# Hybrid MoE step on one core: the samples' rows held as 128 partitions by 256, and half a weight row taken out of the ring

## The chip, the cores and the metric

The kernel runs on one core of one Trainium2 chip. The metric is the device time of one execution in microseconds (us), and lower is better. The kernel before took 1020.41 us, the median of three runs (1020.08 to 1020.62).

## The reference, cut to what matters

There are 288 token rows of 1024 columns: 256 of one prompt and 32 of samples (8 sequences of 4). A mixing layer makes `x`. The expert layer then dominates, with 32 experts whose two weight matrices are 8 MB and 4 MB of float32 each, about 400 MB in all:

```python
logits = xt.astype(jnp.float32) @ router_w.astype(jnp.float32) + router_b.astype(jnp.float32)
vals, idx = lax.top_k(logits, TOP_K)
...
for e in range(N_EXPERTS):
    gu = xt @ w1[e] + b1[e]
    gate = jnp.minimum(gu[:, :D_FF], SWIGLU_LIMIT)
    lin = jnp.clip(gu[:, D_FF:], -SWIGLU_LIMIT, SWIGLU_LIMIT)
    glu = gate * jax.nn.sigmoid(SWIGLU_ALPHA * gate)
    out = (glu * (lin + 1.0)) @ w2[e] + b2[e]
    acc = acc + combine[:, e:e + 1] * out
...
y_prompt = rmsnorm(hp, final_norm_g)
y_sample = rmsnorm(hs, final_norm_g)
```

`rmsnorm(x, g)` is `x * rsqrt(mean(x * x) + eps) * g`, over the 1024 columns of a row.

## The kernel before

Five programs run side by side, one for each engine's queue, and meet at semaphores. SyncE (SP) issues nearly all loads, TensorE (PE) multiplies, ScalarE (ACT) and VectorE (DVE) work on PSUM, GpSimd (POOL) helps at the front and raises the mean square to the power -1/2.

**Front.** The mixing layer ends in `x1_t`, the rows transposed. PE adds up router logits and row sums of squares in four column groups of 32 PSUM partitions (`route`, `add_square`), ACT copies them (`logit_parts`), PE turns the rows back to natural layout (`turn_x1(n, t)`, n the half of the columns, t the tile of rows: 0 and 1 are the prompt, 2 is the 32 samples). The routing chain goes from the logits over DVE, POOL and DVE to `mask`, to the ranks on PE, and to `place_first` on DVE, with which `gather_first` picks rows. Ahead of the ranks PE runs five small matmuls of `keep_awake`. ACT copies the left halves of the turned tiles to `x_acc` (`copy_half`) and makes normed rows (`norm_left`), DVE copies the right halves. `x_acc` is the accumulator of the output: tiles 0 and 1 fill 128 partitions by 1024, tile 2 fills 32 partitions by 1024.

**Pairs.** Experts go in 16 pairs. A w1 block of 512 rows of one expert is a unit of 4 MB: partition p holds its rows 4p to 4p+3, 8 KB each. Four units of 4 MB form `ring`; SP waits on `used` (PE has finished a unit), then loads the next into the freed slot. Within the first pair (`direct`) and the second, PE reports rows and half units (`row_used`, `half_used`), and `load_second` refills in halves. Apart from the ring, rows 0 and 1 of a unit of pair 14 lie in `held` and rows 0 and 1 of one of pair 13 in `late`, both loaded at the front; the ring load of that unit then begins at row 2 (`kept=True`). The front's own ring loads are `load_step(i, a)`: unit i, half a. The last of them, `load_step(3, 1)`, waits until all six `turn_x1` have been done.

A period works on one pair: `first_product` (pairs of 64-column groups in float32), `turn_back` (the places, for the way back), `gather` for the next pair, `second_product` of the pair before. The results of the pair before go back to their rows in six `spread_tile`s: j = 3c + t for half c of the columns and tile t, each two matmuls (`y_high`, `y_low`) of 512 columns into PSUM bank 6 or 7, which DVE adds to `x_acc` (`add_spread`).

**End.** The last units come in halves and column parts (`load_w2_rows`, `load_w2_columns`), then `gain_final` (512 KB, a broadcast of the norm's gain). `finish` on PE seeds PSUM with the four prompt tiles of `x_acc`, runs the last products and returns tiles in `LAST_ORDER` = (0, 1, 2, 5, 3, 4), each in its own bank. ACT squares each tile as it arrives and adds up the row sums; DVE adds the two sample tiles first and multiplies two prompt tiles by the gain (L1791); DVE (L1860) and POOL (L1917) make `rms`; ACT (L1454) and DVE (L1867) scale; six stores go out, the samples' last (L659).

## Time and profile before

| what | value |
|---|---|
| median of three runs | 1020.41 us |
| profiled execution, its own time | 1020.11 us |
| its span, first to last instruction | 1018.4 us |
| granted TensorE clock, mean | 0.985 of full speed |
| PE busy | 952.3 us (94%) |
| DVE, ACT, POOL busy | 311.5, 168.2, 73.5 us |
| read from HBM | 418.62 MB, 413 GB/s over the span |

The profiled execution lies 1.7 us outside its span and 0.30 us below the median. Busy time says how long an engine had work in flight, not whether it set the pace: that is read from what ended its idle time.

### The profile page before, as it was taken

How to read it: one execution, taken by the hardware profiler on the slowest of the kernel's cores; microseconds unless marked ns; L12 is line 12 of the kernel's file. 1: busy time of each engine (PE TensorE's matmuls, PEld its weight loads, DVE VectorE, ACT ScalarE, POOL GpSimd, SP SyncE). 2: the span in 40 equal slices, each digit the busy share in tenths (PEclk: the TensorE clock that was granted, in tenths of full speed). 3: DMA queues.
4: the chain of work that ended last, by engine and by line, in shares of the span. 5: the costliest groups of instructions: out<-in, count | busy, mean ns of one | idle time of the engine just before them, and what ended most of it. 6: DMA issues, size and time to landing. Idle time of an engine off the chain costs nothing.

```text
span 1018.4 us, 12465 instructions
## 1 busy us (share of the span) xinstructions
PE 952.3 (94%) x5216; PEld 428.6 (42%) x5216; DVE 311.5 (31%) x536; ACT 168.2 (17%) x354; POOL 73.5 (7%) x63
## 2 busy tenths in 40 slices
PE   8999999999988998989899898989899899999996
PEld 7999444343333433333243333324243334343332
DVE  5898622131303132231312222121313213131212
ACT  5355612101010101010020101002010101010012
POOL 5985000000000000000000000000000000000000
PEclk9999999999999999999999999999999999999998
DMA  9979999999999999999999999999999999999995
GB/s 322 322 297 411 358 421 437 432 422 435 422 436 425 434 430 430 432 425 437 427 436 431 430 431 424 434 427 435 426 435 432 422 436 423 437 423 433 420 422 202
DMA packets 31189, 420.47 MB, mean 413 GB/s; under 512 B 4219, under 2 KB 4763, under 8 KB 12454
## 3 DMA queue, kind: packets, MB, share of 16 engines
q1 hardware_dynamic: 30651, 418.70, 97.5%
q10 hardware_dynamic: 498, 1.24, 0.3%
q8 instruction: 26, 0.43, 0.2%
q14 instruction: 14, 0.11, 0.0%
HBM read 418.62 MB, written 1.49 MB: 413 GB/s over the span
## 4 chain that ended last, share of the span: by engine, by line
DMA 51%; PE 47%; issue 1%; SPq 0%; DVE 0%; POOL 0%; ACTq 0%; POOLq 0%; ACT 0%; DVEq 0%
DMA ring<-in_exp_w 50%; PE psum L953 22%; PE psum L971 8%; PE psum L760 2%; PE psum L761 2%; PE psum L762 2%; PE psum L1023 1%; PE psum L988 1%; PE psum L859 1%; PE psum L1024 1%; PE psum L794 1%; PE psum L793 1%; PE psum L792 1%; PE psum L842 1%; DMA rows_all<-in_x_sample 1%; PE psum L1006 1%
## 5 line engine op out<-in xcount | busy, mean ns | idle before, releaser
L953 PE MATMUL psum<-ring,rows_all 128*64 128x512 f32 x2016 | 461.6, 607 | 39.8 <-DMA ring<-in_exp_w 39.4
L953 PEld LDWEIGHTS psum<-ring,rows_all 128*64 128x64 f32 x2016 | 139.2, 139 | 316.8 <-issue 259.3
L971 PE MATMUL psum<-ring,rows_all 128*64 128x512 f32 x896 | 199.7, 599 | 13.3 <-DMA ring<-in_exp_w 13.3
L971 PEld LDWEIGHTS psum<-ring,rows_all 128*64 128x64 f32 x896 | 67.8, 138 | 136.4 <-issue 136.1
L1366 ACT ACTIVATE rows_all<-rows_all 128x512 f32<-128x512 f32 x32 | 20.1, 630 | 527.6 <-DVE rows_all L1723 527.6
L1711 DVE TENSOR_TENSOR rows_all<-rows_all,psum 128x512 f32<-128x512 f32 (+1 forms) x84 | 53.6, 678 | 172.2 <-PE psum L1024 172.2
L1740 DVE SCALAR_TENSOR_TENSOR y_low<-psum,gate_of,y_high 128x512 fp32r<-128x512 f32 x32 | 23.7, 751 | 245.8 <-ACT y_high L1374 245.6
L1723 DVE TENSOR_SCALAR rows_all<-psum 128x512 f32<-128x512 f32 x32 | 22.1, 692 | 193.4 <-PE psum L953 193.4
L1914 POOL TENSOR_TENSOR rows_all<-rows_all,held 32x512 f32<-32x512 f32 x1 | 1.3, 1272 | 909.1 <-DVE rows_all L1786 909.1
L1374 ACT ACTIVATE y_high<-psum,gate_of 128x512 fp32r<-128x512 f32 x32 | 22.0, 688 | 217.2 <-PE psum L971 191.0
L859 PEld LDWEIGHTS psum<-place,x_thirds 128*128 128x128 bf16 x744 | 46.6, 97 | 13.0 <-issue 13.0
L859 PE MATMUL psum<-place,x_thirds 128*128 128x128 bf16 x744 | 50.8, 219 | 0.0
L1297 ACT ACTIVATE rows_all<-psum,vecs 128x128 f32<-128x128 f32 x128 | 36.7, 368 | 19.0 <-PE psum L861 13.5
L762 PE MATMUL psum<-x_parts,w_low 128*128 128x288 f32 x128 | 37.7, 295 | 0.0
L1023 PE MATMUL psum<-y_high,back 128*128 128x512 f32 (+1 forms) x84 | 36.4, 433 | 0.0
L1730 DVE SCALAR_TENSOR_TENSOR rows_all<-psum,rows_all 128x512 f32<-128x512 f32 x32 | 33.8, 1056 | 1.1
L1024 PE MATMUL psum<-y_low,back 128*128 128x512 f32 (+1 forms) x84 | 33.1, 394 | 0.0
L1023 PEld LDWEIGHTS psum<-y_high,back 128*128 128x128 f32 (+1 forms) x84 | 13.5, 160 | 37.0 <-issue 34.1
L1902 POOL TENSOR_TENSOR w_low<-ring,w_high 128x512 fp32r<-128x512 f32 x19 | 27.5, 1467 | 13.1 <-ACT w_high L1218 13.1
L861 PE MATMUL psum<-place,samples_thirds 96*128 96x128 bf16 x124 | 27.4, 221 | 0.0
L762 PEld LDWEIGHTS psum<-x_parts,w_low 128*128 128x128 f32 x128 | 24.0, 188 | 0.0
L760 PE MATMUL psum<-x_parts,w_high 128*128 128x288 f32 x80 | 24.0, 300 | 0.0
(263 smaller groups left out, 761.9 us busy)
## 6 DMA issues: line engine op xcount, KB each, us to landing
ring<-in_exp_w SPq DMA_DIRECT2D x53, 4096.0 KB, 30.3
ring<-in_exp_w SPq DMA_DIRECT2D x75, 2048.0 KB, 25.5
ring<-in_exp_w SPq DMA_DIRECT2D x16, 1024.0 KB, 25.5
ring<-in_w_in SPq DMA_DIRECT2D x3, 2048.0 KB, 19.9
ring<-in_w_out SPq DMA_DIRECT2D x1, 4096.0 KB, 12.8
held<-in_exp_w SPq DMA_DIRECT2D x1, 2048.0 KB, 11.8
rows_all<-in_exp_w SPq DMA_DIRECT2D x1, 2048.0 KB, 14.5
ring<-in_exp_w SPq DMA_DIRECT2D x4, 512.0 KB, 21.8
```

Source lines behind the costliest of these rows:

```text
L760: mm(out, w_h, x_h, start=(k == 0), stop=False, skip_group_check=True)
L762: last = mm(out, w_l, x_h, start=False, stop=(k == KD - 1), skip_group_check=True)
L859: mm(out, x_thirds[:, t, part, own], place[:, t], start=(k + t + part == 0), stop=False, skip_group_check=True)
L861: return mm(out, samples_thirds[0:3 * NS, own], place[0:3 * NS, 2], start=False, stop=True, skip_group_check=True)
L953: last = mm(psum[c * SLOTS:(c + 1) * SLOTS, bank, :], gathered_t[:, 4 * kk + j, e, :], weights[:, j, (2 * g + c) * BANK:(2 * g + c + 1) * ...
L971: last = mm(psum[e * SLOTS:(e + 1) * SLOTS, 4 + c, :], h_t[:, 4 * i + j, e, :], ring_w2[:, slot, e, j, c * BANK:(c + 1) * BANK], start=Fal ...
L1023: mm(psum[0:rows[t], 6 + j % 2, :], z, y_high[:, c, :], start=True, stop=False)
L1024: mm(psum[0:rows[t], 6 + j % 2, :], z, y_low[:, c, :], start=False, stop=True).then_inc(spread, 1)
L1297: return A(gathered_t[:, k], src.rearrange("p (e n) -> p e n", e=2), ACT.Copy, scale=vecs[:, G_OWN + k:G_OWN + k + 1])
L1711: V.tensor_tensor(x_acc[0:rows[t], t, c * BANK:(c + 1) * BANK], x_acc[0:rows[t], t, c * BANK:(c + 1) * BANK], psum[0:rows[t], 6 + j % 2, : ...
L1730: V.scalar_tensor_tensor(out=gate_act[:, e, :].rearrange("p (j q) -> p q j", j=4), in0=psum[:, 2 + e, :].rearrange("p (q j) -> p q j", j=4 ...
L1902: G.tensor_tensor(w_low[:, c // KD, c % KD, :], w_in_sb[:, c // KD, c % KD, :], high_buffer(c).bitcast(F32), ALU.subtract).then_inc(w_low_ ...
```

## The change

The samples' 32 rows by 1024 columns are held as 128 partitions by 256: partition 32q + r has columns 256q to 256q+255 of row r (`samples_acc`, in the place of the router weights, `router_g`, once these are used up). PE's four column groups of 32 write them: `return_rows` makes them one tile of a period in place of two, in eight float32 matmuls of 256 columns (four groups, for `y_high` and for `y_low`), so that a period has `SPREADS` = 5 tiles in place of 6. At the front eight more float32 matmuls by the identity put the samples in that form (bank 2), between `turn_x1(0, 1)` and `turn_x1(0, 2)`, and ACT copies them (`copy_groups`) in place of `copy_half(2)`; `x1_turned` counts one more, and DVE copies two right halves in place of three.

The row of 4 KB per partition that `x_acc` gives up becomes `late_half`: half of row 2 of the unit of pair 13 whose rows 0 and 1 are in `late`. It is loaded (512 KB) at the front, behind `logit_parts_ready` and ahead of `load_step(3, 1)`. The ring load of that unit shrinks from 2 MB to 1.5 MB (`load_behind_half`).

At the end the samples' sum of squares is spread over four partitions for each row; one small PE step with `pick_table` adds the four and gives the sum to all four (`samples_meaned`, bank 5). The samples' gain needs its own layout, so four more loads of 32 KB (`gain_samples`) follow `gain_final`; DVE waits for all five before its first use of a gain. POOL no longer multiplies samples by the gain, ACT scales two tiles in place of three, DVE scales the samples first, and their store goes out first.

```diff
         x_norm = rows_all[:, 0:2]
-        x_acc = rows_all[:, 3:6]
+        x_acc = rows_all[:, 3:5]
+        late_half = rows_all[:, 5]
...
+        samples_acc = flat_router[:, 0:QUARTER]
...
+        gain_samples = held[:, 0, D:D + QUARTER]
...
-        LAST_BANKS = (2, 3, 4, 6, 7, 5)
-        LAST_SEEDS = (0, 1, 3, 4)
-        LAST_ORDER = (0, 1, 2, 5, 3, 4)
-        FINAL_DVE = (3, 4, 5)
-        FINAL_ACT = (0, 1, 2)
-        GAINED_DVE = (0, 1)
+        TILES = ((0, 0), (0, 1), (1, 0), (1, 1))
+        SAMPLES = len(TILES)
+        SPREADS = SAMPLES + 1
+        LAST_BANKS = (2, 3, 6, 7, 4)
+        MEAN_BANK = 5
+        LAST_SEEDS = (0, 1, 2, 3)
+        LAST_ORDER = (0, 1, SAMPLES, 2, 3)
+        FINAL_DVE = (2, 3)
+        FINAL_ACT = (0, 1)
...
+            def load_late_half():
+
+                rows = exp_w1[0][PAIRS * 2 - 6, 0:4 * P, :]
+                nc.sync.dma_start(late_half, rows.rearrange("(p j) n -> p j n", j=4)[:, 2, 0:D]).then_inc(late_half_landed, 16)
+
+            def load_behind_half(pair, slot):
+
+                rows = exp_w1[0][bass.ds(pair * 2, 1), 0:4 * P, :]
+                nc.sync.dma_start(ring_flat[:, slot, 5 * D:8 * D],
+                                  rows.rearrange("e (p j) n -> p (e j n)", j=4)[:, 5 * D:8 * D]).then_inc(landed[slot], 16)
...
             load_step(2, 0)
-            sp.wait_ge(x1_turned, 2 * NTILE)
+            sp.wait_ge(logit_parts_ready, 1)
+            load_late_half()
+            sp.wait_ge(x1_turned, 2 * NTILE + 1)
             load_step(3, 1)
...
             nc.sync.dma_start(gain_final, final_norm_g[None, :].to_broadcast([P, D])).then_inc(g_final_landed, 16)
+            for q in range(4):
+                nc.sync.dma_start(gain_samples[q * NS:(q + 1) * NS],
+                                  final_norm_g[None, q * QUARTER:(q + 1) * QUARTER].to_broadcast([NS, QUARTER])
+                                  ).then_inc(g_final_landed, 16)
...
             turn_x1(0, 1)
+            for k in range(2):
+                for q in range(4):
+                    last = mm(psum[q * NS:(q + 1) * NS, GROUPS_BANK, k * P:(k + 1) * P], x1_t[:, 2 * q + k, NP:T],
+                              ident[:], start=True, stop=True, skip_group_check=True)
+            last.then_inc(x1_turned, 1)
             turn_x1(0, 2)
             for t in REST_ORDER:
                 turn_x1(1, t)
-            keep_awake(5, ident[:], bank=7)
+            pe.wait_ge(x_half_copied, 1)
+            keep_awake(5, ident[:], bank=0)
...
+            def return_rows(b, j, bank, start, stop):
+
+                parts = (y_high, y_low)
+                if j == SAMPLES:
+                    for i, y in enumerate(parts):
+                        for q in range(4):
+                            last = mm(psum[q * NS:(q + 1) * NS, bank, 0:QUARTER], back[:, b, NP:T].bitcast(F32),
+                                      y[:, q // 2, (q % 2) * QUARTER:(q % 2 + 1) * QUARTER].bitcast(F32),
+                                      start=start and i == 0, stop=stop and i == 1, skip_group_check=True)
+                    return last
...
                 if end:
                     for n, j in enumerate(LAST_ORDER):
-                        if n % NTILE == 0:
-                            pe.wait_ge(y_low_ready, 4 * h8 - 1 + n // NTILE)
-                        last_tile(1, j, LAST_BANKS[j], start=False, stop=True).then_inc(spread, 1)
+                        if n in (0, 2):
+                            pe.wait_ge(y_low_ready, 4 * h8 - 1 + n // 2)
+                        return_rows(1, j, LAST_BANKS[j], start=False, stop=True).then_inc(spread, 1)
+                    pe.wait_ge(squares, FIRST_SQUARES + LAST_ORDER.index(SAMPLES) + 1)
+                    for q in range(4):
+                        last = mm(psum[q * NS:(q + 1) * NS, MEAN_BANK, 0:1], pick_table[:, 0:E], sumsq[:, 2, 2:3],
+                                  start=True, stop=True, skip_group_check=True)
+                    last.then_inc(samples_meaned, 1)
...
             def finish_last(h8):
                 low_y(h8, 0, y_bank=0)
...
+                dve.wait_ge(g_final_landed, 16 * 5)
+                gain_last(FINAL_ACT[0])
+                dve.wait_ge(spread, 10 * h8 - 9 + LAST_ORDER.index(SAMPLES))
+                V.tensor_tensor(samples_acc, samples_acc, psum[:, LAST_BANKS[SAMPLES], 0:QUARTER],
+                                ALU.add).then_inc(last_added, 1)
+                gain_last(FINAL_ACT[1])
+                dve.wait_ge(samples_meaned, 1)
+                V.tensor_scalar(rms[:, 2, 2:3], psum[:, MEAN_BANK, 0:1], EPS, None, ALU.add)
```

## Rows read from the trace of the kernel before

**Rows 1.** The page: DMA share in tenths and GB/s, in 40 slices of the span

```profile
DMA  9979999999999999999999999999999999999995
GB/s 322 322 297 411 358 421 437 432 422 435 422 436 425 434 430 430 432 425 437 427 436 431 430 431 424 434 427 435 426 435 432 422 436 423 437 423 433 420 422 202
```

**Rows 2.** Windows: width, busy us (count) by engine, clock, DMA share, GB/s

```profile
400.00:500.00 100.00, 91.78 (x456) 34.94 (x458) 21.41 (x38) 9.60 (x22) 0.00 (x0) 1.00 1.00 431
```

**Rows 3.** The page's groups: line, engine, shape, count, busy us, mean ns, idle before

```profile
L953 PE MATMUL psum<-ring,rows_all 128*64 128x512 f32 x2016 | 461.6, 607 | 39.8 <-DMA ring<-in_exp_w 39.4
```

**Rows 4.** Waits of SP's queue: total us, times, longest us

```profile
SPq L503 <- PE psum L953: 256.6, 37, 11.1
```

**Rows 5.** Windows of 2 us at the start of the pairs

```profile
106.00:108.00 2.00, 2.00 (x11) 0.76 (x12) 1.75 (x7) 1.91 (x3) 0.00 (x0) 1.00 0.75 320
108.00:110.00 2.00, 2.00 (x12) 0.57 (x8) 1.56 (x3) 1.97 (x4) 0.00 (x0) 1.00 0.52 111
...
120.00:122.00 2.00, 2.00 (x12) 0.67 (x10) 1.73 (x4) 1.13 (x3) 0.00 (x0) 1.00 0.94 270
```

**Rows 6.** Timeline of SP's queue at the start of the pairs: start, us

```profile
107.97 2.04 SPq L503 DMA_DIRECT2D ring<-in_exp_w  x2
...
119.30 0.33 SPq L503 DMA_DIRECT2D ring<-in_exp_w  x1
```

**Rows 7.** Timeline of PE at the last units

```profile
984.41 3.65 PE L988 MATMUL psum<-ring,rows_all 128*64 128x512 f32 x16 [0.25 <-DMA ring<-in_exp_w]
...
1004.48 0.35 PEld L1006 LDWEIGHTS psum<-ring,rows_all 128*64 128x64 f32 x4 [0.51 <-DMA ring<-in_exp_w]
```

**Rows 8.** Timeline from the last product to the last store

```profile
991.56 4.59 SPq L643 DMA_DIRECT2D held<-in_final_norm_g  x1
...
1007.34 0.75 DVE L1740 SCALAR_TENSOR_TENSOR y_low<-psum,gate_of,y_high 128x512 fp32r<-128x512 f32 x1 [0.91 <-ACT y_high L1374]
...
1010.74 0.57 ACT L1443 ACTIVATE rows_all<-psum 128x512 f32<-128x512 f32 x1
...
1011.43 0.16 DVE L1860 SCALAR_TENSOR_TENSOR rms<-sumsq,sumsq_right 128x3 f32<-128x3 f32 x1 [0.73 <-ACT rows_all L1443]
...
1012.56 1.41 DVE L1867 SCALAR_TENSOR_TENSOR rows_all<-psum,rms,held 128x512 f32<-128x512 f32 x2 [0.96 <-POOL rms L1917]
1013.30 1.55 SPq L649 DMA_DIRECT2D out<-rows_all  x3
...
1014.96 0.77 SPq L659 DMA_DIRECT2D out<-rows_all  x1
```

**Rows 9.** Timeline of the routing chain, PE and DVE

```profile
100.93 1.28 PE L671 MATMUL psum<-ident 128*128 128x128 f32 x10
...
102.17 0.19 PEld L832 LDWEIGHTS psum<-mask,before 128*128 128x128 f32 x1 [0.16 <-DVE mask L1683]
...
103.20 0.56 DVE L1661 TENSOR_TENSOR rows_all<-slot_id,rank 128x384 f32<-128x384 f32 x1
```

**Rows 10.** Timeline: 32 records of four narrow column groups (first and last), and what follows

```profile
150.69 0.31 PE L917 MATMUL psum<-ident,rows_all 128*16 128x128 f32 x3
...
151.47 0.30 PE L917 MATMUL psum<-ident,rows_all 128*16 128x128 f32 x3
151.70 1.09 PE L910 MATMUL psum<-ident,rows_all 128*128 128x128 f32 x8
```

**Rows 11.** A piece of the chain that ended last, at the end: start, us

```profile
1007.47 0.23 PE psum L1094
```

**Rows 12.** Groups by form, 93 to 113 us: count, busy us, mean ns

```profile
L1647 DVE TENSOR_TENSOR ring<-psum,rows_all 128x288 f32<-128x288 f32 x8 | 3.0, 448 | 0.0
```

**Rows 13.** Window at the stores

```profile
1014.00:1016.00 2.00, 0.00 (x0) 0.00 (x0) 0.61 (x1) 0.50 (x1) 0.00 (x0) 0.50 0.93 349
```

**Rows 14.** DMA issues: count, KB each, median us from issue to landing

```profile
bias_rows<-in_exp_b SPq DMA_DIRECT2D x12, 64.0 KB, 2.2
...
held<-in_final_norm_g SPq DMA_DIRECT2D x1, 512.0 KB, 14.1
```

219 lines of the change are left out of this document (113 added, 106 removed).

## Prediction

> **What bounds the kernel now.** I read the page's 40 slices first. The DMA engines are at 9 tenths or more in all slices but two near the front and the last [rows 1]. A window of 100 us in the middle has a DMA share of 1.00 at 431 GB/s, with PE busy for 91.78 us of it [rows 2]. Next I asked what ends PE's idle time: on the w1 products 39.4 of 39.8 us go to loads into the ring [rows 3]. SP's queue for its part waits for PE 37 times at one line, 256.6 us in total [rows 4]. The two don't contradict each other: SP waits for a slot, issues at once, and the load then stands behind others that still keep the DMA engines full. So once the engines are full for good, the end of the loads is fixed by bytes, and neither PE nor DVE work in a period moves it as long as PE keeps up; by the window it has 8 us in 100 in hand.
>
> Three stretches are left. (a) The start of the pairs, where the engines still run dry: their share is 0.75 and then 0.52 in the 4 us from 106 to 110, and 0.94 at 270 GB/s from 120 to 122 [rows 5]. The loads there wait for PE: two are issued from 107.97 on, and the one for the first finished unit at 119.30 [rows 6]. I take 119.30 as the last issue that the engines waited for. What comes before has time to spare; from there on bytes count. (b) The last units: PE waits for a load before 984.41, runs without a gap for about 20 us, and waits once more, shortly, at 1004.48 [rows 7], so its end is tied to the last weights. (c) The chain from the last product to the last store, which no load covers [rows 8].
>
> **The half row that moves.** `late_half` moves 128 x 4096 B = 524,288 B from pair 13, in the full stretch, to the front. At 431 GB/s [rows 2] that is 1.22 us off the full stretch. At the front it is issued behind `logit_parts_ready`, about 97 us, and ahead of `load_step(3, 1)`. It delays that load's end by at most 1.22 us, and behind it the engines idle for 0.25 x 2 + 0.48 x 2 = 1.46 us from 106 to 110 [rows 5], because the next issue comes only with PE at 107.97 [rows 6]. 1.46 is more than 1.22: the move fits into the hole. Term: **-1.22 us**; if the hole is filled by something else, 0.
>
> **The eight matmuls at the front.** They stand between two `turn_x1`, ahead of `keep_awake` and the ranks. PE's five waking matmuls are in flight from 100.93 to 102.21, and the weight load of the ranks begins at 102.17, after 0.16 us of idle that the mask ended [rows 9]. So PE has 0.16 us in hand and no more; `place_first` at 103.20 [rows 9], the first product, and the issues at 107.97 and 119.30 hang on it. The nearest rows to the new work are the cache turns: also float32, 128 columns by the identity, into four column groups. 32 records of them (two for each matmul) fill 150.69 to 151.70, 1.01 us [rows 10]. Sixteen records thus take 0.50 us, and 0.50 - 0.16 leaves **+0.35 us** of delay at 119.30 and so in all that follows. Below: 0, if the waking matmuls overlap more than it seems. Above: a record of full width costs 1.28 / 10 = 0.128 us [rows 9], 2.05 us for sixteen, so +1.9. I take the near row, since it has the very shape. By the Trainium skill, page "TensorEngine Tiling (Array Packing)", section Tiling Modes (Key Properties), a change of the tiling mode drains TensorE. Two more such changes come in here; the turn rows are back to back with full-width work at 151.70 and show no drain that I could price, so the sum has none for it.
>
> ACT has `copy_groups` (256 columns) in place of a copy of 512, which gives some 0.2 us in a place where the mask decides; DVE loses one copy of 0.7 us, behind ACT's normed rows: both 0.
>
> **The periods.** Two sample tiles (4 matmuls of 512 columns) become one of 8 matmuls by 256 in float32. A float32 record of 512 columns runs in pairs at 3.65 us for 16 [rows 7], thus 8 rounds of 0.45; a round of four groups by 256 columns is half that, and four rounds (two records for each of high and low) make 0.9 us. Four records of the old form at 0.23 each [rows 11] make as much. DVE saves one add and a half. Both lie under the full DMA engines: **0**. If this cover were gone, the difference would still be under 0.1 us a period. `load_behind_half` has pieces of 12 KB a partition in place of 16 KB, and nothing in the trace makes them slower.
>
> **The end, up to rms.** All that follows the last weights moves with them. Then: `y_low` for the right half ends at 1007.34 + 0.75 = 1008.09 [rows 8]; the samples' eight matmuls follow and take 0.9, with some 0.2 to the semaphore: 1009.2. DVE's add on 128x256: 0.448 us for 288 columns from PSUM [rows 12], so some 0.42: 1009.7. ACT's square of 256 columns about 0.4: 1010.1; two prompt squares at 0.57 each [rows 8] and reading the sum: 1011.4. Before, the last square started at 1010.74 and L1860 at 1011.43 [rows 8]. Term **0**, between -0.3 and +0.4. The four-partition sum is made meanwhile: square at 1010.1, a tiny PE step, one DVE op, done before 1011.4. Its cover is those two squares, 1.1 us; without them it would cost some 0.5 us.
>
> **The stores.** DVE scales the samples first (256 columns, some 0.45), then two tiles: 1012.56 + 0.45 + 1.41 = 1014.4 in place of 1014.6. SP's first store is issued at about 1013.0 rather than 1013.30, and its last at 1014.5 rather than 1014.96 [rows 8]. In between it is the bytes again: 1.15 MB at 349 GB/s and more, share 0.93 [rows 13]. So not the 0.45 of the last issue counts but nearly the 0.3 of the first: **-0.25 us**, between -0.5 and 0.
>
> **Sum.** -1.22 + 0.35 + 0 + 0 - 0.25 = -1.12 us. Against the profiled execution, 1020.11 us (span 1018.4 and 1.7 around it), that is 1018.99; the median is 0.30 higher, 1020.41, which gives **1019.3 us**. With the bounds that are near the rows (front +0.1 to +0.6, squares and stores as above) the likeliest case spans 1018.4 to 1020.2. A measurement of this kernel tells about 0.2% (2 us) from no change, so this counts as no change.
>
> **Rivals.**
>
> *The move gives nothing net* (the change doesn't do what it says). The front's delay grows to 1.2 us, by drains or by another wait on PE, or the hole at 106 to 110 is no hole for these bytes. For: only 0.24 us of spare room in the hole, and PE has just 0.16 us in hand. Against: the same shape at 1.01 us for 32 records. Time: 1020.41 - 1.22 + 1.2 - 0.25 = 1020.1.
>
> *The column groups don't run side by side* with four different moving operands. The samples' tile then costs 16 records at 0.21 = 3.4 us on the end's path, 2.5 more, and the front +1.9 in place of +0.35. Time: 1019.3 + 2.5 + 1.5 = 1023.3, slower. It decides from two groups at once in place of four. Against: the 32 turn records [rows 10] and the pairs of w1 [rows 7].
>
> *The samples' gain lands late* (the other side too). DVE now waits for five loads before its first multiply by the gain, at about 1008.1. Behind that multiply stand the sample add, the samples' square and two more squares. `gain_final` is issued at 991.56 and lands 14.1 us later [rows 8, 14], at 1005.7. If the four loads landed one behind the other at 2.2 us each, as one 64 KB load of the front takes [rows 14], the last would come at 1014.5, 6.4 us too late: 1019.3 + 6.4 = 1025.7. It decides from 0.6 us for each. For: the broadcast comes at a time when the rate has dropped. Against: the twelve front loads were issued within 8 us (SP's queue), so they overlap; and 128 KB even at the 111 GB/s of the emptiest stretch of rows 5 is 1.2 us, where 2.4 are to spare. [...]
>
> *More than 2 us faster.* The front's delay is 0 and both end terms sit at their lower bound: -1.22 - 0.3 - 0.5 = -2.0, 1018.4; to pass it, something must come that I don't see, such as less idle at 120 to 122. Nothing in the rows speaks for it, but several small terms have one sign.
>
> **Chances.** The likeliest case 0.64; nothing net 0.17; gain late 0.05; groups one by one 0.05; more than 2 us faster 0.09. So faster by over 0.2%: 0.08; within 0.2%: 0.82; slower: 0.10. The range 1018.0 to 1021.2 takes in the first two with the bounds of the unknown costs and leaves out most of the rest.
>
> **What would show it.** In the profile after: DMA share near 1 from 106 to 108; the ranks' weight load at about 102.5 and the next issues at 108.3 and 119.65; the last weights, and PE's last unit, 0.9 us earlier; the sample tile of a period in 0.9 us on PE; L1860's counterpart 0.9 us earlier too; the last store issue 1.3 us earlier. Wrong I'd be if the last weights don't come earlier, if the samples' matmuls follow each other at 0.2 us, or if DVE's first multiply by the gain waits for a load.

## The result and the profile after

The changed kernel takes 1021.21 us, the median of 20 runs (1020.2 to 1024.59), beside 1019.88 us for the kernel before in 20 runs on the same chips: ratio 1.0015, 95% interval 1.0009 to 1.0021. It is 1.3 us slower, a small loss but clear of the noise, since the interval lies wholly above 1; forecast was 1.1 us faster. One of the 20 runs of the kernel before stands apart at 1932.95 us and doesn't move the median; the other 19 took 1019.03 to 1021.86 us. The profiled execution took 1021.2 us, its span 1019.4.

The page's slices for the DMA engines, changed kernel (tenths busy, and GB/s):

```profile
DMA  9879999999999999999999999999999999999994
GB/s 326 322 303 407 366 429 431 431 428 434 422 437 422 435 432 429 432 426 433 426 434 431 433 432 424 438 422 438 424 435 431 422 436 423 435 424 437 417 420 176
```

It is as full as before [rows 1]; the last slice moves 176 GB/s in place of 202. Now the start of the pairs, in three views: windows of 2 us (last two columns DMA share and GB/s), the routing chain, and SP's queue (start, us):

```profile
106.00:108.00 2.00, 2.00 (x12) 0.76 (x12) 1.37 (x6) 1.79 (x3) 0.00 (x0) 1.00 0.94 360
108.00:110.00 2.00, 2.00 (x12) 0.59 (x10) 1.22 (x2) 1.97 (x3) 0.00 (x0) 1.00 0.65 205
120.00:122.00 2.00, 2.00 (x12) 0.72 (x10) 1.73 (x4) 1.13 (x3) 0.00 (x0) 1.00 0.96 303
```

```profile
98.94 0.64 PE L859 MATMUL psum<-ident,ring 128*32 128x128 f32 x16
...
101.28 1.28 PE L702 MATMUL psum<-ident 128*128 128x128 f32 x10
101.63 0.17 DVE L1742 TENSOR_TENSOR mask<-rows_all,logits 32x32 fp32r<-32x32 f32 x1
102.28 0.19 PEld L869 LDWEIGHTS psum<-mask,before 128*128 128x128 f32 x1
...
103.32 0.56 DVE L1720 TENSOR_TENSOR rows_all<-slot_id,rank 128x384 f32<-128x384 f32 x1
```

```profile
108.08 2.04 SPq L514 DMA_DIRECT2D ring<-in_exp_w  x2
...
119.43 0.33 SPq L514 DMA_DIRECT2D ring<-in_exp_w  x1
```

This stretch is as forecast. The hole took the half row: share 0.94 from 106 to 108, where it had 0.75 [rows 5]. Sixteen records fill 98.94 to 99.52, 0.58 us. The waking matmuls now hold the ranks up; these stand 0.11 us later than before [rows 9]. In this execution the load ahead of the routing chain was issued 0.32 us earlier (94.89, before 95.21). I count that as chance and not as part of the change: in the later runs with the changed kernel's front this issue lies anywhere from 94.68 to 95.40 us. So the change costs 0.43 us here, where 0.35 was forecast.

PE at the last units, and from there to the stores (start, us, engine, line; in brackets the idle time before and what ended it):

```profile
984.04 3.65 PE L1033 MATMUL psum<-ring,rows_all 128*64 128x512 f32 x16 [0.27 <-DMA ring<-in_exp_w]
...
1004.34 0.20 PEld L1051 LDWEIGHTS psum<-ring,rows_all 128*64 128x64 f32 x4 [0.68 <-DMA ring<-in_exp_w]
...
1007.76 0.69 DVE L1846 TENSOR_TENSOR rows_all<-psum,held 128x512 f32<-128x512 f32 x1
1007.85 0.16 PEld L1063 LDWEIGHTS psum<-y_high,back 128*32 128x32 f32 x8 [0.89 <-DVE y_low L1802]
...
1009.45 0.42 ACT L1500 ACTIVATE rows_all<-router_g 128x256 f32<-128x256 f32 x1 [1.20 <-DVE router_g L1853]
...
1010.01 0.24 PE L1181 MATMUL psum<-sumsq,pick_table 128*32 128x1 f32 x8
...
1011.14 0.16 DVE L1925 SCALAR_TENSOR_TENSOR rms<-sumsq,sumsq_right 128x2 f32<-128x2 f32 x1 [0.67 <-ACT rows_all L1505]
...
1012.27 0.48 DVE L1928 SCALAR_TENSOR_TENSOR rows_all<-router_g,rms,held 128x256 f32<-128x256 f32 x1 [0.96 <-POOL rms L1978]
...
1012.78 0.74 SPq L683 DMA_DIRECT2D out<-rows_all  x1
1013.57 2.50 SPq L680 DMA_DIRECT2D out<-rows_all  x3
```

L1925 answers to L1860 [rows 8] and is called **the last sum** from here on. Two readings are against the forecast. The last weights end PE's wait only 0.14 us earlier (1004.34, before 1004.48 [rows 7]), and the last sum comes 0.29 us earlier, where 0.9 was forecast and 0.3 is the early front. And from the last sum to the end of the span it takes 1019.4 - 1011.14 = 8.26 us; before it took 1018.4 - 1011.43 = 6.97. The stores lost 1.3 us. Windows of 1 us that begin 2 us behind the last sum, of the kernel before and of the changed one:

```profile
1013.43:1014.43 1.00, 0.00 (x0) 0.00 (x0) 1.00 (x2) 1.00 (x2) 0.00 (x0) 0.50 0.27 102
1014.43:1015.43 1.00, 0.00 (x0) 0.00 (x0) 0.18 (x1) 0.07 (x1) 0.00 (x0) 0.50 1.00 373
1015.43:1016.43 1.00, 0.00 (x0) 0.00 (x0) 0.00 (x0) 0.00 (x0) 0.00 (x0) 0.50 1.04 387
1016.43:1017.43 1.00, 0.00 (x0) 0.00 (x0) 0.00 (x0) 0.00 (x0) 0.00 (x0) 0.50 1.01 318
```

```profile
1013.14:1014.14 1.00, 0.00 (x0) 0.00 (x0) 0.94 (x2) 0.46 (x1) 0.00 (x0) 0.67 0.01 2
1014.14:1015.14 1.00, 0.00 (x0) 0.00 (x0) 0.00 (x0) 0.00 (x0) 0.00 (x0) 0.50 0.42 93
1015.14:1016.14 1.00, 0.00 (x0) 0.00 (x0) 0.00 (x0) 0.00 (x0) 0.00 (x0) 0.50 0.92 318
1016.14:1017.14 1.00, 0.00 (x0) 0.00 (x0) 0.00 (x0) 0.00 (x0) 0.00 (x0) 0.50 1.04 391
1017.14:1018.14 1.00, 0.00 (x0) 0.00 (x0) 0.00 (x0) 0.00 (x0) 0.00 (x0) 0.50 0.93 350
1018.14:1019.14 1.00, 0.00 (x0) 0.00 (x0) 0.00 (x0) 0.00 (x0) 0.00 (x0) 0.50 0.11 41
```

The samples' store is issued first. In the microsecond in which the kernel before already runs at 373 GB/s, the engines here move 93 at a share of 0.42; the pieces of the samples' store started at 1014.11, and the first piece of a tile only at 1014.61.

### The profile page after: what moved, and what is told of

The parts are those of the page before. It is cut to its first block, busy times and chain, and to the rows that moved or that the text cites. A ratio compares the mean times of both kernels' runs of the same rounds, so it can differ in the third digit from the quotient of the medians.

```text
span 1019.4 us, 12866 instructions
## 1 busy us (share of the span) xinstructions
PE 951.8 (93%) x5432; PEld 429.6 (42%) x5432; DVE 298.0 (29%) x521; ACT 166.7 (16%) x351; POOL 72.3 (7%) x62
## 4 chain that ended last, share of the span: by engine, by line
issue 89%; PE 9%; DMA 1%; DVE 0%; ACTq 0%; POOLq 0%; POOL 0%; DVEq 0%
PE psum L791 2%; PE psum L793 2%; PE psum L792 2%; PE psum L825 1%; PE psum L824 1%; PE psum L823 1%; DMA rows_all<-in_x_sample 1%; PE psum L710 0%; PE psum L779 0%; PE psum L800 0%; PE psum L702 0%; POOLq L86 0%; POOL rms L1976 0%; PE psum L769 0%; PE psum L853 0%
## 5 line engine op out<-in xcount | busy, mean ns | idle before, releaser
L1774 DVE TENSOR_TENSOR rows_all<-rows_all,psum 128x512 f32<-128x512 f32 x56 | 36.0, 684 | 120.8 <-PE psum L1070 120.8
L1069 PE MATMUL psum<-y_high,back 128*128 128x512 f32 x64 | 28.5, 445 | 0.0
L1070 PE MATMUL psum<-y_low,back 128*128 128x512 f32 x64 | 25.3, 395 | 0.0
L791 PE MATMUL psum<-x_parts,w_high 128*128 128x288 f32 x80 | 24.0, 300 | 0.0
L792 PE MATMUL psum<-x_parts,w_high 128*128 128x288 f32 x80 | 23.6, 294 | 0.0
```

The lines of the kernel that those rows point to most:

```text
L791: mm(out, w_h, x_h, start=(k == 0), stop=False, skip_group_check=True)
L792: mm(out, w_h, x_l, start=False, stop=False, skip_group_check=True)
L1069: mm(psum[:, bank, :], z, y_high[:, c, :], start=start, stop=False, skip_group_check=True)
L1774: V.tensor_tensor(x_acc[:, t, c * BANK:(c + 1) * BANK], x_acc[:, t, c * BANK:(c + 1) * BANK], psum[:, 6 + j % 2, :], ALU.add).then_inc(spr ...
```

## First experiments: which part costs what

The kernel before stood at 1019.64 us beside these four kernels.

**e0**, the changed kernel again.

> The changed kernel itself, unaltered, timed beside the others on the same chip, as the yardstick for the rest. In its profile the stretch from the start of the last sum of squares on DVE (L1925) to the end of the span was 8.3 us, against 7.0 us for its counterpart before (L1860). Theory 'stores': this 1.3 us is in every execution, so the time is above that of before by 1 us or more. Theory 'rate': the 1.3 us is chance, and the loss comes from slower loads in the full stretch; then this stretch comes out near 7 us here and the last weights land later than before.

Measured: 1021.06 us, 1.0014 (1.0005 to 1.0024). From the last sum to the end 8.27 us again. The last sum itself, though, stood at 1012.73: two executions of one program differ by 1.6 us in the load part. So a difference of 1 us between two profiled executions, outside the stretch of the stores, can't by itself be put down to an edit.

**e1**, the samples' store last:

```
-            sp.wait_ge(final_dve, 1)
-            nc.sync.dma_start(y_sample..., samples_out)      # ahead of the tiles
             ...
             store_half(FINAL_DVE[1])
+            nc.sync.dma_start(y_sample..., samples_out)
```

> Only the order of the stores is changed: the samples' store (128 pieces of 1 KB) goes out last, as in the kernel before, and the three prompt stores of SP ahead of it. Theory 'stores first in small pieces block the rest': L1925 to the end falls from 8.3 to 7.0 to 7.5 us, and the kernel is about 1 us faster than the changed one. Rival 'small pieces cost wherever they stand': the end moves by less than 0.3 us.

Measured: 1021.08 us, 1.0014 (1.0005 to 1.0023); 8.85 us from the last sum to the end. The tiles' stores run at full rate from the start, and then the samples' 128 KB trickle out at 27 to 114 GB/s. So the order isn't the cause: the store is slow at either place. The kernel before stores the same bytes behind its tiles in 32 pieces of 4 KB, which started within 0.43 us (1016.94 to 1017.37); here the 128 pieces of 1 KB started over 2.52 us.

**e2**, the half row not moved (pair 13's unit loaded with 2 MB, no `late_half`):

```
-                load_period(h6, 1, PAIRS - 3, half=True)
+                load_period(h6, 1, PAIRS - 3, kept=True)
...
```

> The half row isn't moved: no load of it at the front, and the unit of pair 13 is loaded with 2 MB as before; all else as in the changed kernel. By the forecast (1.22 us of bytes taken out of the full stretch) this is 1.2 us slower than the changed kernel. Rival 'the front gives it back': the added load at the front delays the loads behind it, and the two are within 0.4 us.

Measured: 1023.1 us, 1.0029 (1.0018 to 1.0041), 1.5 us of ratio over the changed kernel. That is near the 1.2 us of the bytes, but the two intervals overlap, so the size isn't settled by this run.

**e3**, one waking matmul in place of five:

> Ahead of the ranks PE runs one waking matmul in place of five, all else as in the changed kernel. Theory 'the eight matmuls at the front push the ranks': in the changed kernel the ranks' weight load came 0.6 us after the mask; here it follows the mask at once, all loads from the first row on are issued some 0.5 us earlier in relation to the mask, and the kernel is 0.3 to 0.5 us faster. Rival 'the front's delay is absorbed': no change over 0.1 us, or slower if the clock falls.

Measured: 1021.01 us, 1.0011 (1.0002 to 1.0020). The front's delay is gone (the issue at 108.08 now at 107.91, although this front began 0.26 us later), which is 0.4 us in the profile and can't be told in the times.

## Second experiments: rows, bytes, order

The kernel before stood at 1019.75 us.

**e4**, the first store of the end takes other data, 32 partitions of 4 KB:

```
-            nc.sync.dma_start(y_sample.rearrange("b t (q n) -> q (b t) n", q=4), samples_out)
+            nc.sync.dma_start(y_sample.rearrange("b t d -> (b t) d"), gain_final[0:NS, :])
```

> The changed kernel, but the first store of the end takes its 128 KB from 32 partitions of 4 KB each (the final gains' copy) in place of 128 partitions of 1 KB each; so the samples' output is not the samples' result, and all that computes it is still done. Theory A (the 1.3 us lost at the end are the price of the 128 short rows of the samples' store): from the last sum of squares' instruction (the counterpart of L1925) to the end of the span takes 7.0 to 7.3 us, as the 6.97 of before, where the changed kernel took 8.26; the third store's issue is back from 1.55 us to about 0.45; the time is 1.0 to 1.3 us under the changed kernel, ratio to before 1.0001 to 1.0005. Theory B (the four stores of the prompt's tiles are as slow without it, because the stores of SP and ACT now start closer together): the stretch stays at 8.0 us or more, the ratio at 1.0014.

Measured: 1021.42 us, 1.0019 (1.0010 to 1.0028), and 8.3 us from the last sum to the end. Theory A, as I had it, fell: with long rows nothing was won, although the third tile's issue did come back from 1.55 to 0.45 us. But the shape of the tail was another one.

**e5**, no load of the half row at the front; its products take the second kept row:

```
-            load_late_half()
...
-                period(h6, 1, kept=(late, late_landed, 4), half=late_half)
+                period(h6, 1, kept=(late, late_landed, 4), half=late[:, 1])
```

> The changed kernel without the 512 KB load of the half row at the front; the unit of pair 13 is still loaded without it, and the half row's products take other weights (the second row of those loaded at the front), so that these products are not the reference's. Theory A (the half row's load is free: it lies in a stretch in which the queues have nothing else due): the same time as the changed kernel, ratio to before 1.0014. Theory B (it takes the place of other loads' packets, and puts the slowest DMA engine further behind): 0.5 to 1.2 us under the changed kernel, ratio 1.0002 to 1.0009, the full load of the last slot issued at about 108 lands 0.5 to 1.2 us earlier against its issue.

Measured: 1020.61 us, 1.0011 (1.0002 to 1.0020). Against 1.0014 and 1.0015 that is not told from nothing; the median would fit theory B too, at its lower edge.

**e6**, the kernel before with the shorter load alone:

> The kernel before, with nothing of the change but the shorter load of pair 13's first unit: 1.5 MB in place of 2 MB; the products of the half row left out take other weights (the second row of those loaded at the front), so that these are not the reference's. It is the move's gain alone, without the price of a load at the front, of the samples' new form or of the short stores. Theory A (512 KB less in the full stretch are worth their time at its rate, 430 GB/s): 1.2 us under before, ratio 0.9988. Theory B (landings go by the slowest of the 16 DMA engines, which has slack to lose or gain elsewhere): under 0.6 us, ratio 0.9994 to 1.0000.

Measured: 1018.52 us, 0.9989 (0.9980 to 0.9999): 1.23 us of median, with an interval of 0.1 to 2.0 us. That agrees with the first term of the forecast's sum, 1.22, but doesn't prove its size: in the profiled execution the last sum came 1.73 us earlier, and a part of that has another source (the lag, below).

**e7**, the samples' root apart and early, and one waking matmul (the lines on GpSimd; VectorE's waits follow suit):

```
...
+            pool.wait_ge(samples_eps, 1)
+            G.tensor_tensor(rms[:, 2, 2:3], rms[:, 2, 2:3], half[:, 2:3], ALU.pow).then_inc(samples_rooted, 1)
             pool.wait_ge(rms_ready, 3)
```

> The changed kernel with two edits: the samples' root is taken by GpSimd by itself as soon as their mean is there, so that their scaling and store go ahead of the last sum of squares and of the root for the prompt's rows; and one waking matmul in place of five at the front. Theory A (the price of the short rows is time on the DMA engines and on SP ahead of the tiles' stores, and can be hidden before them): the samples' store is issued at 0.7 to 0.9 us after the last sum (L1925's counterpart) in place of 1.64, the stretch from that sum to the end is 7.0 to 7.5 us in place of 8.26, and the time 0.9 to 1.3 us under the changed kernel: ratio to before 1.0001 to 1.0006. Theory B (the short rows cost the end wherever their store stands, as when it was put last): 8.0 us or more, ratio 1.001.

Measured: 1020.89 us, 1.0007 (0.9998 to 1.0016). The samples' store was issued 0.58 us behind the last sum, as hoped, and the end still took 8.4 us. Theory B by the number, and once more with another shape.

That shape was the way on. Each store's landing is counted up by each DMA engine that took part, so the records show when each engine is done. From the last sum, in us:

```
                        all but three   last but one   last   span's end
before                       6.49           6.52       6.53      6.97
changed                      7.68           7.71       7.82      8.26
e0 changed again             7.69           7.72       7.83      8.27
e1 samples last              7.82           8.27       8.38      8.85
e4 long rows                 6.54           7.23       7.85      8.30
e7 samples early             6.60           7.34       7.95      8.40
```

Before, the last store's landings end at 6.53 us. In the changed kernel most of the last 16 come at 6.99 to 7.38, and five landings at 7.62 to 7.82: every engine is late, and a few are later still. In e4 and e7 they are in time as before, but for two landings, 0.7 and 1.3 us behind the rest. The packets of that time run one at a time, six of about 80 ns in each 0.5 us, which fits one engine with its pieces of two stores still to move (the records don't name the engine). So there seem to be two causes, and either hides the other.

## Third experiments: a branch that fetches code

What that engine may carry besides is in the DMA part of the trace, which gives each queue. Packets of the stores' stretch, 1012 to 1020, changed kernel (queue and kind: packets, MB, share):

```profile
DMA packets 709, 1.20 MB, mean 150 GB/s; under 512 B 68, under 2 KB 196, under 8 KB 708
...
q1 hardware_dynamic: 564, 0.92, 33.0%
q10 hardware_dynamic: 144, 0.26, 9.0%
q8 instruction: 1, 0.02, 0.8%
```

```
before    1008.15 COMPARE_BRANCH 3.70 L1173   q8 packets at 1009.1 (1.36 us) and 1012.6 (1.33)
changed   1010.03 COMPARE_BRANCH 3.65 L1228   q8 packets at 1011.0 (1.32 us) and 1014.6 (0.98)
```

Behind its last product PE jumps over the code of the further rounds (`with nc.tensor.Else()`) to the end of the program. That code isn't there yet: the branch takes 3.7 us, with one packet in it and one behind it. The jump comes when PE has passed its last wait. Before, that was `y_low`; in the changed kernel it is the samples' square (L1500), for PE's new step L1181. So the second packet lies 1.2 us behind the last sum in one, ahead of the stores, and 3.5 us behind it in the other, among them.

The kernel before stood at 1020.13 us.

**e8**, the kernel before with one wait more on PE, behind its last tile:

```
                 finish(HALF - 1, HALF, end=True)
+                pe.wait_ge(squares, LAST_SQUARES - 2)
```

> The kernel before, with one more wait on TensorE after its last tile and ahead of its last branch: for the second of the last four squares by count, which comes 1.2 us ahead of the last sum, as the samples' mean does in the changed kernel. Nothing else waits for TensorE there. Theory C (TensorE's last branch jumps over the code of the further rounds, and the code behind it is fetched in two packets of 16 KB on one DMA engine; the second of them lies ahead of the stores in the kernel before, and among them in the changed one, because there TensorE still does the samples' mean): the second packet moves from about 1.2 us behind the last sum (L1860's counterpart) to about 3.4 us behind it, one engine's pieces of the stores land about 1 us after the others', the stretch from the sum to the end is 7.7 to 8.3 us in place of 6.97, and the time is 0.8 to 1.2 us over before: ratio 1.0008 to 1.0012. Theory A (short rows alone lengthen the stores): no difference, ratio 1.0000.

Measured: 1020.95 us, 1.0010 (1.0001 to 1.0019), and 8.7 us from the last sum (1010.27) to the end, where the kernel before takes 6.97. Nothing but PE's jump was put later. Its windows, from 2 us behind the last sum:

```profile
1012.27:1013.27 1.00, 0.00 (x0) 0.00 (x0) 1.00 (x2) 1.00 (x2) 0.00 (x0) 0.52 0.26 98
1013.27:1014.27 1.00, 0.00 (x0) 0.00 (x0) 0.18 (x1) 0.07 (x1) 0.00 (x0) 0.50 1.08 383
1014.27:1015.27 1.00, 0.00 (x0) 0.00 (x0) 0.00 (x0) 0.00 (x0) 0.00 (x0) 0.50 0.97 354
1015.27:1016.27 1.00, 0.00 (x0) 0.00 (x0) 0.00 (x0) 0.00 (x0) 0.00 (x0) 0.50 0.50 188
1016.27:1017.27 1.00, 0.00 (x0) 0.00 (x0) 0.00 (x0) 0.00 (x0) 0.00 (x0) 0.50 0.61 148
```

```profile
1013.60 2.19 SPq L659 DMA_DIRECT2D out<-rows_all  x1
```

The code packet, at 1013.3, ran 1.69 us. The issue of the last store, begun meanwhile, took 2.19 us in place of 0.77 [rows 8], and its 128 KB came only after a gap, from 1016.3. The two last landings came at 8.05 and 8.35, all but three by 7.14. The stretch is above the 7.7 to 8.3 us of theory C and the median only 0.8 us over before: in the profiled execution the load part was 0.8 us shorter (the lag again).

**e9**, the changed kernel with PE's last two arms exchanged, so that the jump is taken near 965:

```
-            with nc.tensor.If(more < 1):
-                finish(HALF - 1, HALF, end=True)
-            with nc.tensor.Else():
+            with nc.tensor.If(more >= 1):
                 with nc.tensor.Fori(1, ROUNDS) as r:
                 ...
+            with nc.tensor.Else():
+                finish(HALF - 1, HALF, end=True)
```

> The changed kernel, with the two arms of TensorE's last branch exchanged: the further rounds stand in the first arm, the usual end in the second, so that the jump is taken ahead of the last two units, near 965, and the code behind the usual end follows it without a jump. Theory C with A beside it (the fetch and the short rows overlap, and either alone is enough for most of the loss): no packet of code among the stores, and the stretch from the last sum to the end is 7.6 to 8.2 us, against 8.26; the time 0 to 0.6 us under the changed kernel. Theory C alone: 6.9 to 7.2 us, 1.2 us under it. In both the jump costs TensorE about 3.7 us near 965, where it has idle time in each unit, and the six slots ahead of it should keep the loads going; if they don't, the last weights land up to 3 us later.

**e10**, the same with e4's long rows.

> The previous edit, and the first store of the end takes 32 partitions of 4 KB in place of 128 of 1 KB (from the final gains' copy, so that the samples' output is not the samples' result). Theory C with A beside it: both causes are gone, the stretch from the last sum to the end is 6.9 to 7.2 us in place of 8.26, and the time is 1.0 to 1.4 us under the changed kernel: ratio to before 0.9999 to 1.0005. If a third cause holds the stores, 8 us as with the long rows alone.

**e11**, the same exchange in e7's kernel.

> The kernel with the samples' root and store ahead of the last sum and one waking matmul, and the exchanged arms of TensorE's last branch: all of the computation is done. Theory C with A beside it (the short rows go out while nothing else is stored, and no code is fetched among the stores): no engine's pieces land late, the stretch from the last sum to the end is 6.9 to 7.3 us (8.4 with the samples early alone), and the time is 1.1 to 1.5 us under that kernel: 1019.3 to 1019.8 us, ratio to before 0.9994 to 1.0001. Theory A (short rows cost the end wherever they stand): 8 us or more.

Measured, from the last sum to the end: e9 8.18 us, e10 6.94, e11 6.98. Their last landings: 7.71, 6.55, 6.61. This is theory C with A beside it to 0.1 us: with the slow store alone the end stays long, with the code packet alone (e4, e7) too, and with neither it is as short as before. The windows of e10, with neither:

```profile
1014.56:1015.56 1.00, 0.00 (x0) 0.00 (x0) 0.94 (x2) 0.46 (x1) 0.00 (x0) 0.50 0.61 131
1015.56:1016.56 1.00, 0.00 (x0) 0.00 (x0) 0.00 (x0) 0.00 (x0) 0.00 (x0) 0.50 0.82 309
1016.56:1017.56 1.00, 0.00 (x0) 0.00 (x0) 0.00 (x0) 0.00 (x0) 0.00 (x0) 0.50 1.02 385
1017.56:1018.56 1.00, 0.00 (x0) 0.00 (x0) 0.00 (x0) 0.00 (x0) 0.00 (x0) 0.50 0.91 342
1018.56:1019.56 1.00, 0.00 (x0) 0.00 (x0) 0.00 (x0) 0.00 (x0) 0.00 (x0) 0.50 0.03 12
```

The times don't follow: 1022.18 us (1.0022, 1.0013 to 1.0031), 1021.69 (1.0017, 1.0006 to 1.0027) and 1020.16 (1.0001, 0.9992 to 1.0010). The jump near 965 took 6.1 us, more than the 3.7 that I expected, and brought three code packets into the stretch of full rate within 12 us. What that does to the loads is the next part.

## Fourth experiments: the load part, and a mean off TensorE

Each load too is counted by its 16 engines. In the stretch of full rate the slowest of them lands behind the middle one (the eighth of 16) by a time that stays the same for hundreds of microseconds. This **lag** then jumps, up or down, by 0.5 to 1.7 us about where a code packet lies: in the kernel before from 0.8 to 2.0 us behind the packet at 276.6, in the changed one from 2.3 to 2.9 behind the one at 294.6. PE waits for the slowest. Below, the lag of the load that landed between 981.9 and 985.7 us, and the time from SP's issue at about 119.3 to the last sum, in profiled executions:

```
                        lag    issue to last sum   less the lag
before                  2.0        892.13             890.1
e8  before, late jump   1.2        891.31             890.1
e2  changed, no move    3.5        893.61             890.1
e6  before, short load  1.1        890.43             889.3
changed                 2.8        891.71             888.9
e0  changed again       4.1        893.50             889.4
e1                      2.4        890.91             888.5
e3                      2.5        891.28             888.8
e4                      2.5        891.93             889.4
e5                      1.7        891.25             889.6
e7                      1.7        891.60             889.9
e13 changed, shifted    2.1        891.28             889.2
```

Less the lag, the kernels that load the half row in the stretch of full rate agree at 890.1, and those that don't stand at 888.5 to 889.9, 0.2 to 1.6 us lower and 0.9 in the mean. So the half row's gain seems to be there in the changed kernel too, and in its profiled execution 0.8 us of it went into a larger lag. The column was worked out after the fact, from one execution of each kernel, and the lag isn't settled at that point: it rose from 2.6 to 4.1 us in e0 and from 2.0 to 3.5 in e2 between two loads about 6 us apart, and in e7 from 1.7 to 3.0 with the next load. With the jump near 965 the same sum gives 889.7 (e9), 889.2 (e10) and 890.5 (e11), the last outside the rule.

The kernel before stood at 1019.80 us.

**e12** and **e13**, the kernel before and the changed one, with their code shifted:

```
             pe.wait_ge(consts_made, 1)
-            keep_awake(8, ident[:])
+            keep_awake(4, ident[:])
+            for _ in range(64):
+                pe.wait_ge(consts_made, 1)
```

> The kernel before, with 64 waits that are already met put on TensorE at the very start, in place of four of its eight first waking matmuls: all its later code stands some 60 instructions further on in its 16 KB blocks. Theory L (the place of the code packets against the loads decides how far the slowest DMA engine lags): the slowest engine's lag behind the median in the loads around 980 differs from 2.0 us by 0.3 or more in either direction, and the time follows by about as much, up to 0.8 us: ratio 0.9992 to 1.0008. Theory N (the place is of no consequence, the lag comes from the kernel's own loads): the lag is 1.9 to 2.1 us again and the ratio 1.0000.

> The same in the changed kernel. Theory L: the lag around 980 differs from 2.8 us, and the time from the changed kernel's by up to 0.8 us either way: ratio to before 1.0006 to 1.0022. Theory N: lag 2.7 to 2.9 us and ratio 1.0014.

Measured: e12 1022.27 us, 1.0023 (1.0014 to 1.0031), lag 3.1 us, issue to last sum 893.16, less the lag 890.1. e13 1022.43 us, 1.0029 (1.0018 to 1.0039), lag 2.1 us. The 64 waits, on PE 1000 us ahead of the end, leave the issue near 119.3 later by 0.34 and 0.6 us. The kernel before became 2.5 us slower in the median; in its profiled execution (1021.57 us) the last sum came 1.37 us later, of which 0.34 is the start's and 1.1 the lag's. Shown is that this edit, 1000 us ahead of the end, costs 2.5 us, which is outside both theories' ratios. Theory L fits the direction, but its cause isn't shown: the lag is read in one execution, and e0 against the changed kernel has a difference in lag of 1.3 us with no edit at all. For the changed kernel the lag of one execution fell by 0.7 us while the median rose by 1.4 over the earlier runs, so there the profile and the times don't even have one sign.

**e14**, the same with 128 waits.

> The same with 128 such waits, half a block. The start is about 1 us later if the waits take more than the four matmuls that they replace. Theory L: another lag again, and the packets of the stretch of full rate come some 5 to 12 us earlier than in the changed kernel. Theory N: as the changed kernel, but for what the start costs.

Measured: 1025.45 us, 1.0050 (1.0037 to 1.0063). The loads issued at 82.16 us in the changed kernel went out at 87.93, so the time is set by the front; the lag around 984 was 2.1 us.

**e15**, all of the computation, without PE in the samples' mean:

```
-                    pe.wait_ge(squares, FIRST_SQUARES + LAST_ORDER.index(SAMPLES) + 1)
-                    for q in range(4):
-                        last = mm(psum[q * NS:(q + 1) * NS, MEAN_BANK, 0:1], pick_table[:, 0:E], sumsq[:, 2, 2:3], ...)
...
+                for q in range(4):
+                    last = V.tensor_copy(flat_sums[0:NS, q:q + 1], sumsq[q * NS:(q + 1) * NS, 2, 2:3])
+                then(last)
+                then(V.reduce_sum(flat_sums[0:NS, 4:5], flat_sums[0:NS, 0:4], axis=AX.X))
+                for q in range(4):
+                    last = V.tensor_scalar(rms[q * NS:(q + 1) * NS, 2, 2:3], flat_sums[0:NS, 4:5], EPS, None, ALU.add)
```

> The whole computation. The samples' mean is summed over the four column groups by VectorE in nine small operations in place of TensorE's four matmuls, so that TensorE's last wait is that for y's low part, as in the kernel before, and its last branch starts 2.2 us earlier against the last sum; the samples' root and store go ahead of the prompt's; of the samples' matmuls those on y's first half, and those on the high part of its second, are issued ahead of the wait for its low part; one waking matmul at the front. Theory C with A beside it: the second code packet is at about 1.2 us behind the last sum, the stretch from that sum to the end is 7.0 to 7.3 us, the last sum itself comes 0.3 to 0.45 us earlier against the last weights' landing, and the time is 1.2 to 1.7 us under the kernel with the samples early alone: ratio to before 0.9990 to 0.9997. If VectorE's nine operations hold the last sum up, 0.2 to 0.5 us of it are lost.

Measured: 1019.50 us, 0.9999 (0.9990 to 1.0007), 1.6 us under the changed kernel's ratio and level with the kernel before. The code packet stands 1.2 us behind the last sum, as in the kernel before. From the last sum to the end it took 7.6 us, not 7.0 to 7.3: the samples' root holds GpSimd when the prompt's is due (0.17 us), and all landings but three come at 7.14. Of the two slow causes the store itself is left.

## Last experiments: the store on four engines

**e16**, e1's kernel with the samples' store cut in four, and **e17**, e15's with the same (two stores ahead of the tiles, two behind):

```
-            nc.sync.dma_start(y_sample.rearrange("b t (q n) -> q (b t) n", q=4), samples_out)
...
+                for q in quarters:
+                    nc.sync.dma_start(y_sample.rearrange("b t d -> (b t) d")[:, q * QUARTER:(q + 1) * QUARTER],
+                                      samples_out[q * NS:(q + 1) * NS])
```

> The changed kernel with the samples' store behind the tiles', as in the earlier run with that order, but in four stores of 32 rows by 1 KB: the same 128 pieces in the same place. Theory D (the one store went to 4 of the 16 DMA engines, because its outermost dimension is 4): each of the four stores leaves 16 semaphore packets; the last landings but three come 6.4 to 7.0 us behind the last sum, against 7.82 with the one store, and the stretch from the sum to the end is 7.2 to 8.3 us (its upper part if the code packet's engine is last) against 8.85. Theory A (pieces of 1 KB are slow as such): 7.8 or later, and 8.8 us or more, since three more issues are added.

> The whole computation: the kernel with the samples' mean off TensorE, and the samples' rows in four stores of 32 rows, two ahead of the prompt's stores on SyncE's queue and two behind them. Theory C with D: no engine has more to carry than the others, the stretch from the last sum to the end is 7.0 to 7.2 us against 7.62, and the time is 0.4 to 0.6 us under that kernel: ratio to before 0.9990 to 0.9997. Theory A: 7.6 us or more, ratio 0.9999 or over.

The DMA part for the stores of e1 (one store) and of e16 (four), with the same 128 pieces of 1 KB in the same place:

```profile
DMA packets 709, 1.20 MB, mean 133 GB/s; under 512 B 68, under 2 KB 196, under 8 KB 708
```

```profile
GB/s 0 0 0 0 0 0 0 0 0 0 254 352 377 377 360 426 361 360 369 377 352 221 58 131 41 144 45 139 16 25 0 0 0 0 0 0 0 0 0 0
DMA packets 769, 1.20 MB, mean 120 GB/s; under 512 B 128, under 2 KB 256, under 8 KB 768
```

The times didn't gain, and D's forecasts of the end were missed. e16: 1022.14 us, 1.0023 (1.0013 to 1.0032), 9.1 us from the last sum to the end where D said 7.2 to 8.3, all landings but three at 7.98 where it said 6.4 to 7.0; e17: 1020.09 us, 1.0004 (0.9995 to 1.0013), 8.0 us where it said 7.0 to 7.2. By these numbers alone theory A would have been right, with a reason that the packets' times refute. In e16 all landings but five came by 7.55 us, and the last five followed 0.2 us apart, to 8.60, as on one engine put back by the code packet at 1015.9. What the four stores cost besides is issue time, as SP's queue shows in e17:

```profile
1010.18 1.81 SPq L681 DMA_DIRECT2D out<-rows_all  x2
1012.04 1.43 SPq L687 DMA_DIRECT2D out<-rows_all  x3
1013.51 1.66 SPq L681 DMA_DIRECT2D out<-rows_all  x2
```

A pair of stores of 32 KB takes SP 1.66 to 1.81 us to issue, some 0.9 each, twice the 0.45 of a tile's 256 KB. The last one leaves SP 6.1 us behind the last sum, when most bytes of the others are through. So no run here has the samples' form on 16 engines without that price, and how much of the 1.3 us goes with the four engines is known only through the long rows (e9 against e10, 8.18 and 6.94 us). Those also shorten the store's own issue, from 0.74 to 0.33 us. No version here that does the whole computation beats the kernel before; e15 is level with it.

## Why the prediction was wrong

**The step that failed first** is **The stores**, "-0.25 us, between -0.5 and 0": measured +1.3 in both profiled executions of the changed kernel. The first issue and the bytes were right (1012.78, forecast about 1013.0), but the tiles' three issues began at 2.42, 2.89 and 3.37 us behind the last sum, before at 1.87, 2.28 and 2.94, and the last of them took 1.55. What I took as given was that the bytes go out at the rate of [rows 13] in any form. Two things took its place, each enough for nearly all of it alone (e9 8.18 us, e4 8.3, both together 8.26): the samples' store used 4 engines, took longer to issue, and the tiles behind it came late (all but three landings at 7.68 for 6.49); and PE's new step at the end made its last jump 2.2 us later against the last sum, so that a 16 KB code packet fell among the stores (e8: +1.8 from the last sum to the end in the profile, +0.8 in the median, with nothing else changed). The first I could have read in the diff, where the outermost dimension is 4. The second I treated only as "a tiny PE step" that squares cover; I asked what waits for it, and not what PE does behind it.

**The half row**, -1.22: not contradicted as a term, and not proved in size. e6 gives -1.23 of median for the shorter load alone and e2 against the changed kernel 1.5, both with wide intervals (0.1 to 2.0 us for e6); less the lag the profiles give 0.9 in the mean. The hole at 106 to 108 took the load; e5 finds no price that can be told. But the gain didn't arrive: from the issue at 119 to the last sum the changed kernel is only 0.42 us shorter in the profiled pair (891.71 for 892.13).

**The eight matmuls**, +0.35: right, 0.43 measured, for the reason given.

**The periods**, 0: the samples' tile takes 0.9 to 1.0 us on PE, near the forecast (at 431.71 eight records in 0.64 us, at 432.17 eight in 0.61, the next product at 432.71), and the rate is 430 GB/s as before. This is the second step that failed. What it left out is that "the end of the loads is fixed by bytes" holds for the engines together, while PE waits for the slowest of them. The lag was 2.8 us in place of 2.0 in the profiled execution, 0.8 us of the gain. Whether the changed kernel has it larger in general is open: over its variants it was 1.3 to 4.1 us, and 4.1 in the same program a second time. The "8 us in 100 in hand" are also those of one window: from 800 to 900 PE was busy for 98.07 us before and 99.25 after, so its cover is thinner there than I took it to be. And of the 40 slices one near the front and the last are under 9 tenths, not two and the last.

**Up to rms**, 0: right. From the last weights (1004.34) to the last sum 6.80 us; before 6.95.

**Rivals.** The column groups run side by side: 16 records in 0.58 us at the front, 0.08 more than the cache turns gave, so no drain over 0.1 us shows. The gain is in time: DVE's L1846 starts at 1007.76 behind its own work, and the last landing of the five loads stands at 1006.24. The four small loads were issued from 995.53 to 997.37 and didn't wait for each other: on the engine that came last their pieces started 0.09 us apart, at 1005.06 to 1005.33. "Nothing net" comes nearest in its number (1020.1) and not in its reason. A loss by the stores was not among the rivals.

The account: +0.43 front, -0.9 to -1.2 half row, +1.3 stores, together +0.5 to +0.8, against +1.3 measured (0.9 to 2.1 by the interval). The 0.5 to 0.8 us left are the size of the lag's difference in the profiled executions; with a lag that changes from run to run I don't call this shown. In the profiled pair itself the spans add up: +0.13 us to the issue at 119, -0.42 from there to the last sum, +1.29 behind it, together the 1.0 us by which the spans differ.

## What to carry to other kernels

Look at the outermost dimension of each transfer on both sides before its bytes: 4 there meant 4 engines of 16 here, and in the trace such a transfer shows by its count of landing packets. Cutting it up buys the engines back at the price of more issues. Ask of a step added at a program's end what its engine does behind it: here a far jump fetched code over an engine that carried the last stores. When a change removes one cause of a late end and nothing moves, look at the shape of the landings and not only at the last one: two causes can hide each other.

## What the runs showed of the hardware

- PE's jump to code that wasn't there took 3.3 to 3.8 us with the loads over, and 6.1 us among loads at full rate (e9 to e11).
- A code packet is 16 KB on one DMA engine, 0.9 to 1.7 us long; PE's straight code brings one every 19 to 31 us of the last periods.
- At 430 GB/s the slowest of 16 engines stayed behind the middle one for hundreds of microseconds, by 1.2 (e7) to 3.4 us (e12), and by 1.1 (e6) to 4.1 (e0) at the loads around 984; PE waited for it.
- 64 more waits on PE at the start, already met, made the kernel before 2.5 us slower in the median, of which the start's own were 0.34 us in the profiled execution.
- A store that used 4 engines also held the third issue behind it: 1.55 us in place of 0.47 before, in e9 too, where no code packet was near.
- Pieces of 1 KB took 55 to 57 ns each, on 4 engines and on 16 (the changed kernel and e16).
